# A two-block decoder layer on one core: the order in which the first x tiles, the first weight tiles and the norm columns are fetched, and a second weight group taken tile by tile

## The reference, cut to what matters

```
h    = rmsnorm(x, norm_mix_g)          # x * rsqrt(mean(x*x) + eps) * g
proj = h @ w_in                        # 1024 x 5384
lru_x, lru_gate, m_qk, m_v, m_o, m_i, m_f, s_q, s_k, s_v, g_a, g_b, g_c = split(proj)
```

## Time and profile before

| | |
|---|---|
| median of 3 runs | 749.52 us (749.52 to 749.61) |
| profiled execution | 749.77 us, of which the span of the core 748.0 us |
| TensorE busy | 740.5 us (99%), 4280 matmuls |
| VectorE, ScalarE, GpSimd busy | 523.8, 402.5, 49.7 us |
| chain that ended last, by engine | TensorE 97%, VectorE 2% |
| granted TensorE clock | 1.00 in all slices |

### The profile page before, as it was taken

How to read it: one execution, slowest core, us unless ns; L and a number is a source line. 1 busy time by engine, 2 the same in 40 slices (tenths; PEclk the granted TensorE clock), 3 DMA queues, 4 the chain that set the end, 5 groups by cost and what they waited for, 6 DMA issues and landing times.

```text
span 748.0 us, 10384 instructions
## 1 busy us (share of the span) xinstructions
PE 740.5 (99%) x4280; PEld 648.8 (87%) x4280; DVE 523.8 (70%) x612; ACT 402.5 (54%) x509; POOL 49.7 (7%) x71
## 2 busy tenths in 40 slices
PE   9999999999999999999999999999999999999996
PEld 9988888889988888888899898789988988888885
DVE  6788946885766666656779998785758655556564
ACT  6678378544545545444653685673647443454442
POOL 0200002120000000000230200030003000000000
PEclk9999999999999999999999999999999999999999
DMA  9866365555565556666466536365065466555431
GB/s 337 280 224 225 137 237 210 171 171 168 176 219 169 170 171 204 215 203 209 154 218 205 165 117 225 116 235 165 21 212 166 162 221 225 172 199 188 162 123 57
DMA packets 74239, 138.42 MB, mean 185 GB/s; under 512 B 3916, under 2 KB 28368, under 8 KB 74064
## 3 DMA queue, kind: packets, MB, share of 16 engines
q1 hardware_dynamic: 72336, 132.69, 52.9%
q10 hardware_dynamic: 1856, 5.06, 1.9%
HBM read 136.69 MB, written 1.05 MB: 184 GB/s over the span
## 4 chain that ended last, share of the span: by engine, by line
PE 97%; DVE 2%; issue 0%; ACT 0%; DVEq 0%; ACTq 0%
PE wide L2074 70%; PE bank L2074 25%; PE bank L2198 2%; DVE low L1318 0%; DVE arena L1581 0%; ACT arena L723 0%; DVE act_hl L1415 0%; DVE xn L1809 0%; DVE x L1819 0%; DVE arena L1641 0%; DVE arena L1637 0%; DVE hid_l L1646 0%; DVE arena L1643 0%; DVE arena L1627 0%; DVEq L263 0%
## 5 line engine op out<-in xcount | busy, mean ns | idle before, releaser
L1318 DVE TENSOR_TENSOR low<-raw,high 128x2048 fp32r<-128x2048 f32 (+1 forms) x118 | 267.0, 2279 | 106.2 <-ACT high L723 101.5
L723 ACT ACTIVATE high<-raw 128x2048 fp32r<-128x2048 f32 (+3 forms) x134 | 234.7, 1770 | 122.8 <-PE wide L2074 95.9
L2074 PE MATMUL wide<-act_hl,high 128*128 128x256 f32 (+1 forms) x1184 | 241.3, 327 | 0.0
L2074 PEld LDWEIGHTS wide<-act_hl,high 128*128 128x128 f32 x1184 | 198.9, 191 | 18.3 <-issue 0.2
L2074 PE MATMUL wide<-high,act_hl 128*128 128x512 f32 x528 | 170.1, 394 | 0.5 <-DVE arena L1581 0.2
L2074 PE MATMUL wide<-act_hl,low 128*128 128x256 f32 x832 | 161.2, 284 | 0.0
L2074 PEld LDWEIGHTS wide<-act_hl,low 128*128 128x128 f32 x832 | 128.6, 192 | 2.8 <-DVE low L1366 0.2
L2074 PEld LDWEIGHTS wide<-high,act_hl 128*128 128x128 f32 x528 | 99.1, 188 | 23.3 <-issue 1.7
L2074 PE MATMUL wide<-low,act_hl 128*128 128x512 f32 x264 | 103.0, 390 | 0.0
L2074 PE MATMUL bank<-high,hid_l 128*128 128x512 f32 x216 | 84.4, 391 | 0.3 <-DVE hid_l L1646 0.3
L2074 PE MATMUL bank<-low,hid_h 128*128 128x512 f32 x216 | 84.2, 390 | 0.0
(11 more groups left out here) (215 smaller groups left out, 681.1 us busy)
## 6 DMA issues: line engine op xcount, KB each, us to landing
raw<-in_w_ff_dram SPq DMA_DIRECT2D x32, 1024.0 KB, 5.3
raw<-in_w_in_dram SPq DMA_DIRECT2D x27, 1024.0 KB, 5.3
raw<-in_w_ffn_in_dram SPq DMA_DIRECT2D x44, 512.0 KB, 4.9
raw<-in_w_ffn_out_dram SPq DMA_DIRECT2D x11, 1024.0 KB, 6.5
raw<-in_w_xkv_dram SPq DMA_DIRECT2D x8, 1024.0 KB, 5.0
raw<-in_w_o_dram SPq DMA_DIRECT2D x4, 1024.0 KB, 5.1
raw<-in_w_out_dram SPq DMA_DIRECT2D x4, 1024.0 KB, 5.0
raw<-in_w_xq_dram SPq DMA_DIRECT2D x4, 1024.0 KB, 5.2
```

The lines of the kernel that those rows point to most:

```text
L723: return act.activation(dst, src, func, **k)
L1318: tt(part(low, g), part(raw, g), f32(part(high, g)), SUB).then_inc(sem.low_by_dve, 1)
L2074: return pe.matmul(dst, lhs, rhs, start=start, stop=stop, skip_group_check=loose)
```

## The change

The first four groups are now fetched and split tile by tile (`FINE` = 4). SyncE's head order becomes: left half of weight tile 0, weight tile 1, x tile 2, weight tile 2, x tile 3, weight tile 3, and so on to x tile 7 and weight tile 7, tiles 8 to 11, then tiles 12 to 15 one by one, then x by tokens, `vec`, `if_bias`, `gate_w`. ScalarE's queue issues `first_x`, the right half of weight tile 0, x tile 1. There are twelve semaphores `first_in`, and tiles 12 to 15 use the first four a second time; tiles 2 to 7 wait for 32, their x tile and their weight tile. Tile 12 goes into the buffers of group 0, so its high and low part wait for `w_used` >= 1. `rep_made` stands before K tile 6 of qk.

```diff
-        FINE = len(chunks["lru"]) + 1
-        first_in = [... for k in range(4 * FINE)]
+        FINE = len(chunks["lru"]) + len(chunks["qk"])
+        first_in = [... for k in range(12)]
...
+        def first_count(kt):
+
+            mine = 32 if 2 <= kt % 12 < KD else 16
+            return mine if kt < 12 else mine + 16
...
-                if g == FINE + 1:
+                if g == FINE:
                     sp.dma_start(x[:, :, :], w["x"].rearrange("(t p) d -> p t d", p=P)).then_inc(sem.x_in, 16)
-                if g == FINE + 1:
+                if g == FINE:
+                    sp.dma_start(vec[:, :], w["vecs"]).then_inc(sem.vec_in, 16)
                     sp.dma_start(if_bias[:, :], w["if_bias"]).then_inc(sem.bias_in, 16)
...
                             sp.dma_start(tile[:, 0, 0:T], src[row:row + P, c:c + T]).then_inc(sem.first_half_in, 16)
-                            sp.dma_start(tile[:, 0, T:NB], src[row:row + P, c + T:c + NB]).then_inc(first_in[0], 16)
                             continue
+                        if 2 <= g * n + k < KD:
+                            kt = g * n + k
+                            sp.dma_start(x_t[:, kt:kt + 1, :], w["x_t"][:, kt - 1:kt, :]).then_inc(first_in[kt], 16)
                         sp.dma_start(tile[:, k, :], src[row + k * P:row + (k + 1) * P, c:c + cw])\
-                          .then_inc(first_in[g * n + k], 16)
-                        if g < 2 and k % 2 and g * n + k + 1 < KD:
-                            k0 = g * n + k + 1
-                            sp.dma_start(x_t[:, k0:k0 + 2, :], w["x_t"][:, k0 - 1:k0 + 1, :]).then_inc(first_in[k0], 16)
+                          .then_inc(first_in[(g * n + k) % 12], 16)
...
                 act.dma_start(first_x[:, :], w["first_x"]).then_inc(sem.first_x_in, 16)
+                (src, row, n, d, c, cw), = groups[0][0]
+                act.dma_start(part(raw, 0)[:, 0, T:NB], src[row:row + P, c + T:c + NB]).then_inc(first_in[0], 16)
                 act.dma_start(x_t[:, 1:2, :], w["x_t"][:, 0:1, :]).then_inc(sem.x_t_in, 16)
-                act.dma_start(vec[:, :], w["vecs"]).then_inc(sem.vec_in, 16)
...
-                elif kt % 2 == 0:
+                else:
                     act.wait_ge(first_in[kt], 32)
...
-                act.wait_ge(first_in[kt], 32 if 2 <= kt < KD and kt % 2 == 0 else 16)
+                act.wait_ge(first_in[kt % 12], first_count(kt))
+                if kt == 12:
+                    act.wait_ge(sem.w_used, 1)
...
                 dve.wait_ge(sem.first_high, kt + 1)
+                if kt == 12:
+                    dve.wait_ge(sem.w_used, 1)
...
-            products("qk", "C", at={5: rep_made})
+            products("qk", "C", at={6: rep_made})
```

More of the change, by code:

```diff
@@ L422, in two_blocks @@
         sem = Semaphores(lambda name: ctx.enter_context(nc.semaphore(name)))
-        FINE = len(chunks["lru"]) + 1
-        first_in = [ctx.enter_context(nc.semaphore(f"first_in{k}")) for k in range(4 * FINE)]
+        FINE = len(chunks["lru"]) + len(chunks["qk"])
+        first_in = [ctx.enter_context(nc.semaphore(f"first_in{k}")) for k in range(12)]
         raw_in = [ctx.enter_context(nc.semaphore(f"raw_in{s}")) for s in range(RAW)]
```

## The result

The changed kernel takes 750.87 us (median of 19 runs, 750.2 to 752.04), the kernel before 749.52 us (19 runs, 749.06 to 750.07). The ratio is 1.0018, with a 95% interval of 1.0011 to 1.0024: slower by 1.35 us. That is clear of the noise, and just inside the 1.5 us that the prediction had called no change. The forecast was 750.4. The profiled execution took 750.95 us, its span 749.2.

A forecast was written before the change was run, and what follows sets the result against it. TensorE, busy 99%, was taken as the bound, VectorE's chain close behind. One K tile later 1.44, less diagonal wait 0.18, head 0.34, slack 0.06: + 0.86 us on 749.52 gives 750.4; case 750.0 to 750.8, range 748.9 to 751.1.

The forecast's parts named there:

- the range of its case: Whole kernel: late `rep_out` delays VectorE's chain and vo, and the delay lasts to the end; median 750.0 to 750.8 us.
- TensorE without pause from 4.70: Sign that the forecast is right: TensorE runs without a pause from 4.70 us to the end of qk.
- + 1.20 less the head's gain: General form of the total delay, carried from vo to the end: + 0.86 to + 1.20 us.
- the head's gain: TensorE at the head: pauses before K tiles 2 and 3 given back, 0.34 us, bounds 0 and 0.34.
- Right half of weight tile 0 on ScalarE's queue: Head transfers: takes x tile 1's place, costs nothing if landed before 5.2 us; each 0.1 us late costs 0.1.
- Tile 2 needs no wait: TensorE at the head: K tile 2's high part is ready near 7.9 us, K tile 1 ends about 8.5.
- Transfers by bytes, not by issue: x by tokens: issued 2 to 2.5 us later, but landing stays 21.4 less 0.2, plus at most 0.3 us.
- The rival with x late: x by tokens lands up to 2.5 us later if issues set its landing: + 2.4 us, 751.9; chance 0.07.
- The advice of the Trainium skill to batch: Group 3: 1 MiB batching advice would make four 256 KB transfers cost more; forecast expected 380 GB/s, hardly below later rate.
- VectorE's idle stretch: Sign that the forecast is right: VectorE idles 0.6 to 0.7 us before the lru drain.
- The pauses are saved and kept: Rival: VectorE's chain has unseen slack and vo starts when TensorE arrives: - 0.52 us, 749.0; chance 0.15.
- Half rate ends sooner: Rival: first eight matmuls run at 0.12 us each, saving 0.9 us, with pauses 1.4, with warm-up 1.5: 747.9; chance 0.04.

The follow-up runs named there:

- Experiment 1: The changed kernel with `rep_made` back before K tile 5 of qk: 749.55 us against 749.64 for the kernel before.
- experiment 2: The kernel before with only `rep_made` moved, to before K tile 6 of qk: 750.98 us against 749.64.
- experiment 3: The changed kernel with VectorE's lru convolution moved behind group 6's low part: 749.34 us against 749.64 for the kernel before.
- experiment 4: The changed kernel with weight tile 0's right half back on SyncE's queue, x tile 1 second on ScalarE's: 750.43 us against 749.64 for the kernel before.
- experiment 5: The changed kernel, unaltered, executed once more for its trace: 750.94 us.
- experiment 10: The kernel of experiment 9 with group 3 fetched and split whole again: 749.35 us against 749.46 for the kernel before.
- experiment 9: The changed kernel with weight tile 0's right half back on SyncE's queue and lru's convolution behind group 6's low part: 749.33 us against 749.46 for the kernel before.
- experiment 7: The changed kernel with weight tile 0's right half back on SyncE's queue and `rep_made` before K tile 5: 749.65 us against 749.54 for the kernel before.
- experiment 6: The kernel before with only lru's convolution on VectorE moved behind group 6's low part: 749.52 us against 749.54.
- experiment 8: The changed kernel with the half tile back on SyncE, `rep_made` before K tile 5, lru's convolution behind group 6's low part: 749.2 us against 749.54 for the kernel before.

## Why the prediction was right, and where it was off

**Mechanism.** It was right: the path turns from TensorE to VectorE at vo, because `rep_out` comes late and everything behind it on VectorE is in a fixed order. Experiment 1 removes the cost with the one index, experiment 2 produces all of it with the same index, and experiment 3 removes it by taking the convolution out of the chain. The sum came out short, though. The prediction gave 750.0 to 750.8 as the range of its case, and 750.87 lies just outside it, inside the wider 748.9 to 751.1. Of the signs named, "TensorE without pause from 4.70" failed: its weight loads pause for 0.22 us before K tile 1.

**The form of the sum.** "+ 1.20 less the head's gain" held. The changed kernel's passes begin at 26.50. With the old pace and no gain they would have begun at 26.42. So the gain was - 0.08, the sum gives + 1.28, and vo moved by 1.27. In experiment 4 the gain in the trace was 26.42 - 25.64 = 0.78; the sum gives + 0.42, and vo moved by 0.41. The median of its 11 runs, + 0.79, stands for a gain of about 0.4: that trace was faster at the head than the median run.

**The term that was mis-sized.** It is the head's gain, put at 0.34 and measured at - 0.08. By the same reckoning it is 0.11 in experiment 3 and 0.10 in experiment 5, so it is nothing within what traces differ by. The kernel of experiment 2, with the old head, has its passes at 26.48 and the same time. The step that failed is "Right half of weight tile 0 on ScalarE's queue": it said that the half tile took the place of x tile 1, and priced only the half tile's landing. It did not price x tile 1 in its new place behind it, nor ScalarE's rounding of the half tile after its landing. The view of the transfers had what was needed. These are ScalarE's second and third transfer in the kernel before (KB each, us from issue to landing):

```profile
arena<-in_x_t_dram ACTq DMA_DIRECT2D x1, 128.0 KB, 3.2
...
vec<-in_vecs_dram ACTq DMA_DIRECT2D x1, 75.0 KB, 4.7
```

And this is x tile 1 as the third in the changed kernel:

```profile
arena<-in_x_t_dram ACTq DMA_DIRECT2D x1, 128.0 KB, 4.6
```

Issued at 1.71, the third place meant a landing near 6.4 by the row of before; ScalarE had it at 6.38. The prediction's "Tile 2 needs no wait" was true but no help, since K tile 1 had become the late one. The other transfers of the new head did bring something: experiment 10 has them with the half tile back on SyncE's queue, at the pace of the kernel before (2.04 us for the first eight), and its passes begin at 25.91, a gain of 0.51.

**Transfers by bytes, not by issue.** This was right. x by tokens was issued 1.24 us later (11.95 against 10.71) and landed 0.6 us earlier: its first square is at 20.80, with 21.2 to 21.5 expected. In the other traces with this head or experiment 4's it is at 20.70 to 21.48, so the 0.6 us is no gain that can be counted on. The rival with x late falls. The issue came 2 to 2.5 us later in the prediction, and that count was off: before, SyncE had nothing to issue from 8.83 to 10.29, where it waited for the low part of tile 3, and five issues more mostly filled this gap. The advice of the Trainium skill to batch (DMA: Bandwidth & Descriptors, Bandwidth) would have group 3 move faster whole, as in experiment 10, than in four tiles, as in experiment 9. No run shows that here: x by tokens, behind group 3 on the same queue, is there at 20.75 and 20.70, and the medians are 749.35 and 749.33.

**VectorE's idle stretch** was 1.39 us and not 0.6 to 0.7. It was longer at both ends: `rep` came 0.35 us later, and group 4's low part ended 0.39 us sooner (at 26.01), since the diagonal in front of it was ready sooner and its own high part too. It is the end that counts.

**The rivals.** "The pauses are saved and kept" fell in experiment 7: a saved pause ends at vo unless the chain is relieved too. "Half rate ends sooner" did occur as an event (below), but not as the change's doing: it is in the traces of experiments 2 and 6, with the old head, as well. Where VectorE's chain holds vo it is waited away, as in experiment 2.

What stays open: how often the wait at 60 us takes the gain of experiments 9 and 10. It was read in one trace of each, once with the wait and once without. Their medians lie 0.13 and 0.11 us under the kernel before, and that of experiment 8 0.34 us; the intervals, over 1 us wide, tell none of these apart. Open too is what makes group 7's transfer take 8 us or 5 (below). No version here is faster than the kernel before by more than its interval.

## What to carry to other kernels

When an engine's program is a fixed order, moving a short instruction on another engine can hold a long queue behind it: ask what waits for its result and what stands behind that waiter. Four passes placed one K tile later cost 1.3 us, because the drain that needs them stands in front of the work that a later product needs. And a transfer put into a queue moves every transfer behind it: price the one pushed back as well as the one that was moved.

## What the runs showed of the hardware that was not expected

The pace of the first real matmuls (256 columns each, from 4.6 us on) differs from trace to trace. The first eight took 2.04 us in the kernel before and in experiment 10, 2.26 in the changed kernel, where two of them wait for the half tile by 0.22 us together, 2.08 and 2.02 in experiments 1 and 3, 1.76 in 8, 1.44 in 4, and 1.19 in 2, 6, 7 and 9. TensorE's instructions up to there are the same in all. Laid out one by one, the starts of matmuls that follow without a wait are 0.213 us apart up to a moment and 0.117 to 0.12 us behind it. That moment is 6.75 us in the kernel before, 7.1 in the changed one, 5.15 in experiment 4, and 4.0 to 4.2, still in the warm-up, in 7 and 9. Read with the clock's two levels, 0.213 us is 256 columns at 1.2 GHz, one per cycle, and little more than half of it is the level of 2.4 GHz. The granted clock reads 1.00 throughout. But the record behind that column begins only within 0.1 us of this moment (6.74 us in the kernel before, 5.14 in experiment 4), and the view shows the stretch without a record as 1.00. So a 1.00 at the start of a kernel has to be checked against the pace of the matmuls. Experiment 2, which ran at the upper level from the start, gained nothing by it: K tile 1 waited 0.64 us for its weights.

The second surprise is the time that group 7, one transfer of 1 MB on SyncE's queue, took to land. It was 8.1 us in the kernel before, beside 4.9 for group 6 just ahead of it, and over the twelve traces it falls into two sets. Behind `rep_out` ScalarE issues another transfer, `row_g` (512 KB, one row of 4 KB written to all 128 partitions). In seven traces, those of the kernel before and of experiments 1, 4, 6, 7, 8 and 9, `row_g` is issued up to 1.0 us ahead of group 7 or together with it, and group 7 takes 7.5 to 8.5 us. In the other five, those of the changed kernel and of experiments 2, 3, 5 and 10, `row_g` is issued at least 0.5 us behind group 7, and group 7 takes 4.9 to 5.9 us. No run moved `row_g` by itself, so that it is the cause is not shown. In experiment 9 this landing set the path: its faster head brought `rep_out`, and with it `row_g`, up to the moment of group 7's issue (25.98 beside 25.95).
